# Gated recurrence: the next head's row projection placed between the last two half-size products, and the first head's ScalarE and VectorE work in another order

## What is computed

```
def c_layer(x, s0, w_in, norm_g, w_out, lb):
    q, f, i, g = jnp.split(jnp.einsum('btd,de->bte', x, w_in).astype(jnp.float32), 4, axis=-1)
    q = jax.nn.silu(q).reshape(B, T, H_C, C_DK)
    logf = jnp.logaddexp(jnp.log(lb), jnp.log1p(-lb) + jax.nn.log_sigmoid(f)).reshape(B, T, H_C, C_DK)
    k = -jnp.expm1(logf)
    v = i.reshape(B, T, H_C, C_DV)
    o, s_new = gla_chunked(q, k, v, logf, s0.astype(jnp.float32))
    o = o * lax.rsqrt(jnp.mean(jnp.square(o), axis=-1, keepdims=True) + RMS_EPS)
    o = o.reshape(B, T, D_MIX) * norm_g.astype(jnp.float32) * jax.nn.silu(g)
    return jnp.einsum('bte,ed->btd', o.astype(x.dtype), w_out), s_new
```

## Time and profile before

| | |
|---|---|
| median of 3 runs | 2076.14 us (2073.19 to 2078.51) |
| the profiled execution's own time | 2070.61 us |
| its span, first to last instruction | 2068.5 us |
| mean granted TensorE clock | 0.977 |
| TensorE busy | 1959.7 us, 95% of the span |
| VectorE, ScalarE, GpSimd busy | 1050.3, 773.6, 385.2 us |
| first and last row projection (L2254) | start at 1278.2 and 1884.2 us |

### The profile page before, as it was taken

How to read it: one execution, slowest core, us unless ns; L and a number is a source line. 1 busy time by engine, 2 the same in 40 slices (tenths; PEclk the granted TensorE clock), 3 DMA queues, 4 the chain that set the end, 5 groups by cost and what they waited for, 6 DMA issues and landing times. The chain is left out here.

```text
span 2068.5 us, 46493 instructions
## 1 busy us (share of the span) xinstructions
PE 1959.7 (95%) x19082; PEld 1470.9 (71%) x19082; DVE 1050.3 (51%) x2617; ACT 773.6 (37%) x1687; POOL 385.2 (19%) x424
## 2 busy tenths in 40 slices
PE   7999999989998999997997998899999999999998
PEld 7888888856666877875665444777888788788533
DVE  3211131158874444435774243667777877777332
ACT  0000011168774444342776010345445544544300
POOL 5432333336650000003541100000000000000000
PEclk9999999999998999998999998999999999999999
DMA  6334323453149999986663914499998998998730
GB/s 180 103 119 95 78 66 82 71 140 105 50 162 322 399 379 386 387 346 236 226 245 117 294 22 122 146 293 295 319 308 277 310 311 281 305 311 298 236 126 26
DMA packets 221953, 443.39 MB, mean 214 GB/s; under 512 B 60816, under 2 KB 182176, under 8 KB 205104
## 3 DMA queue, kind: packets, MB, share of 16 engines
q1 hardware_dynamic: 214288, 364.57, 55.0%
q0 software_dynamic: 7456, 75.86, 10.0%
HBM read 413.70 MB, written 165.23 MB: 280 GB/s over the span
## 5 line engine op out<-in xcount | busy, mean ns | idle before, releaser
L2264 PE MATMUL three<-x1T,arena 128*128 128x256 f32 x768 | 207.0, 397 | 3.7 <-DVE rec_qq L2655 3.7
L580 POOL TENSOR_TENSOR late<-late 128x512 f32<-128x512 f32 (+2 forms) x76 | 112.2, 1476 | 219.4 <-PE pab_bZ L368 126.4
L2563 POOL TENSOR_TENSOR rec_v_own<-rec_rows,row_own 64x512 f32<-64x512 f32 x16 | 16.6, 1040 | 729.7 <-PE rec_bX L2379 598.1
L2264 PEld LDWEIGHTS three<-x1T,arena 128*128 128x128 f32 x768 | 137.4, 193 | 19.1 <-DVE rec_qq L2655 4.1
L848 ACT ACTIVATE ap_sc<-ap_sc,ap_nmax 128x256 f32<-128x256 f32 (+1 forms) x192 | 106.3, 557 | 5.1 <-DVE ap_nmax L872 5.0
L1456 DVE COPY sa_kT<-sa_bT 128x512 f32<-128x512 f32 x80 | 55.2, 690 | 94.5 <-PE sa_bT L1312 94.4
L872 DVE CUSTOM_DVE_ANT_0 ap_sc<-ap_bS,ap_bias 128x256 f32<-128x256 f32 (+1 forms) x192 | 86.2, 486 | 14.0 <-DMA ap_bias<-in_bias_p 9.6
L907 POOL TENSOR_SCALAR ap_sc<-ap_sc,ap_rden,sgl 128x256 f32<-128x256 f32 (+3 forms) x128 | 76.8, 612 | 40.0 <-DVE ap_rden L880 39.7
L1456 ACT COPY sa_kT<-sa_bT 128x512 f32<-128x512 f32 x80 | 46.9, 586 | 98.8 <-PE sa_bT L1312 98.6
L1475 DVE COPY sa_xT<-sa_bT 128x512 f32<-128x512 f32 x64 | 43.8, 684 | 64.9 <-PE sa_bT L1377 64.5
L2264 PE MATMUL three<-rec_T,arena 128*128 128x256 f32 x256 | 63.8, 392 | 8.8 <-DVE rec_gg L2655 8.3
(11 more groups left out here) (505 smaller groups left out, 4583.4 us busy)
## 6 DMA issues: line engine op xcount, KB each, us to landing
out<-in_cache_a_k SPq DMA_DIRECT2D x8, 8160.0 KB, 30.0
out<-in_cache_a_v SPq DMA_DIRECT2D x8, 8160.0 KB, 29.6
arena<-in_cache_a_k SPq DMA_DIRECT2D x40, 1024.0 KB, 8.5
arena<-in_cache_a_v SPq DMA_DIRECT2D x40, 1024.0 KB, 9.1
arena<-in_w_in_c SPq DMA_DIRECT2D x64, 512.0 KB, 6.7
late<-in_w_in_ab SPq DMA_DIRECT2D x128, 64.0 KB, 2.4
late<-in_w_in_ab SPq DMA_DIRECT2D x8, 1024.0 KB, 5.3
ap_bias<-in_bias_p SPq DMA_DIRECT2D x16, 512.0 KB, 3.9
```

The source lines that it names most:

```text
L580: nc.gpsimd.tensor_tensor(to, a, b, op).then_inc(sums, 1)
L2264: last = nc.tensor.matmul(bank[:, 0:SEQ // 2], left[:, k, :], right[:, k, :], start=(first and k == 0), stop=(k == 3), skip_group_check=True)
L2563: nc.gpsimd.tensor_tensor(v_own[:, :, :], sV[h % 2].unsqueeze(1).broadcast_to([TS, HALF_NB, P]), row_own[:, :].unsqueeze(2).broadcast_to([ ...
```

## The change

Three edits, all in `recurrence`. TensorE does `project_rows(h + 1)` in iteration h, between A21 x B12 and A22 x T4 of `values_and_gates`, rather than at the start of iteration h+1; only `project_rows(0)` stays at a start. ScalarE does the first Exp (with its wait for `lb_ready`) behind the first head's side copy rather than ahead of everything. VectorE does, in the first head alone, the fifth `add`, then `set_constants`, then `forget`.

```diff
@@ values_and_gates
                     product(A21, B12, bR[0], True)
+                    if h + 1 < HC:
+                        project_rows(h + 1)
                     pe.wait_ge(added, ADDS * h + 9)
                     product(A22, T4, bR[0], False)
@@ TensorE's loop over the heads
-                    if before:
+                    if h == 0:
                         project_rows(h)
-                    else:
+                    if not before:
                         pe.wait_ge(added, ADDS * HC)
@@ ScalarE
                 act.wait_ge(const_ready, 16 * 6)
-                act.wait_ge(lb_ready, 1)
-                nc.scalar.activation(lb[:, :], one_lb[:, :], ACT.Exp).then_inc(lb_ready, 1)
                 line = Line(act, act_line)
@@
                         nc.scalar.copy(side[h % 2][:, :], bS[:, TS:4 * TS]).then_inc(side_read, 1)
+                        if h == 0:
+                            act.wait_ge(lb_ready, 1)
+                            nc.scalar.activation(lb[:, :], one_lb[:, :], ACT.Exp).then_inc(lb_ready, 1)
@@ VectorE
                         add(h, 4, 6, bR[0], qq[:, T_2], qq[:, T_2])
+                        if h >= 1:
+                            forget(h)
+                        dve.wait_ge(added, ADDS * h + 3)
+                        add(h, 5, 7, bR[0], qq[:, T_1], qq[:, T_1])
                         if h == 0:
                             set_constants()
-                        forget(h)
-                        dve.wait_ge(added, ADDS * h + 3)
-                        add(h, 5, 7, bR[0], qq[:, T_1], qq[:, T_1])
+                            forget(h)
                         forget_rest(h)
```

## The result

The changed kernel took 2116.99 us (median of 4 runs, 2109.74 to 2121.61) against 2074.8 us before (median of 4, 2073.19 to 2078.51). The ratio is 1.0198, with a 95% interval of 1.0179 to 1.0217: slower by some 41 us by the ratio, 42 by the medians. The profiled execution took 2109.74 us, with a span of 2107.6 us and a mean granted clock of 0.978; that is 39.1 us over the profiled execution of before in time and in span alike.

What follows compares the result with a forecast made beforehand. The prediction took TensorE to bound the steady heads. The profiled 2070.6 us plus 37.1 for 14 seams and 0 for the first head gave 2107.7; from the median 2076.1 it gave 2113 us, range 2103 to 2128.

Steps and rivals of the forecast that it cites:

- Step 1: At each seam the moved row projection waits 0.77 us for the bank ScalarE empties, replacing the old 0.52 us wait.
- Steps 2 and 3: At each seam A22 x T4 runs 3.85 us later and the tenth add 3.27 us later; S1 x T1 waits 1.20 us.
- Step 4: At each seam turn_values, no longer covered by the row projection, waits 1.20 us for ScalarE's logarithm.
- The sum of a seam: S1 x T1 starts 2.65 us later per head, at 14 seams: +37.1 us.
- The first head: Both small edits, their clock price and the seam from head 0 to 1: sum +0.4, taken as 0.
- -6.6: In the first head both edits together bring S4 x B22 from 1315.45 to about 1308.9.
- The worked gain of the two edits: First head: -3.8 us from the late Exp, -2.8 from the set-up order, +3.0 for low clock; -3.6 us.
- the first seam: From head 0 to 1 the tenth add and S1 come later, +2.3 us, with +1.7 us charged for low clock.
- The clock price behind the long wait: In the first head, +3.0 us for low clock behind a wait of some 5 us ahead of S4 x B22.
- The clock: Rival: three short waits per seam bring TensorE's clock down, +23.8 us at all 14 seams, 2137 us; chance 0.13.
- Sums not the last: Rival: at the seams only turn_values and turn_side wait, 1.48 us per head, +20.7 us: 2097 us; chance 0.04.
- The bubble is covered and nothing is late: Rival: the moved rows fill the 0.52 us wait, VectorE's late start is absorbed: faster, 2064.7 us; chance 0.03.

Runs made afterwards that it cites:

- bank_early: The whole change, with ScalarE's copy of the sample outputs moved ahead of the two exponentials: 2101.33 us against 2075.03 before, ratio 1.012.
- sums_early: The whole change, with VectorE making the next head's S1, S2 and S4 ahead of the tenth add: 2092.67 us against 2075.03 before, ratio 1.0078.
- turns_late: `sums_early` with TensorE doing turn_values behind A11 x B11 and turn_side behind S1 x T1: 2077.07 us against 2075.85 before, ratio 1.0.
- first_only: The whole change with the row projection put back, so only the first head's two edits: 2070.66 us against 2075.03 before, ratio 0.9976.
- exp_late: The kernel before with ScalarE's edit (the later Exp) alone: 2076.1 us in one execution, beside 2080.53 before.
- setup_late: The kernel before with VectorE's edit (fifth add, set_constants, forget) alone: 2071.99 us in one execution, beside 2080.53 before.
- all_early: `turns_late` with the early copy of the sample outputs of `bank_early`: 2064.54 us against 2075.85 before, ratio 0.9934.
- after_again: The changed kernel unaltered, measured once more: 2116.24 us against 2075.85 before, ratio 1.0183.

## Why the prediction was right, by its steps

**What bounds the kernel.** TensorE did, and each microsecond by which its work comes later at a seam was a microsecond of time. Seams of 42.64, 41.71, 41.35, 40.26, 39.72, 39.35 and 39.29 us go with ratios of 1.0183, 1.012, 1.0078, 1.0, 0.9976, 0.9934 and 0.9917. From the start of the recurrence to the last S1 x T1 the traces of these kernels differ from before by +39.6, +26.7, +16.7, +1.5, -5.3, -9.7 and -11.2 us (single stalls of TensorE that no other engine ends left out); the ratios give +38, +25, +16, 0, -5, -14 and -17. The last two agree less well than the others.

**Step 1, the rows' start.** Predicted a wait of 0.77 us for ScalarE's copy of the sample outputs; 0.85 measured, and taking it away gave back 0.93 us per seam (`bank_early`). ScalarE's copy starts 1616.56 - 1614.15 = 2.41 us behind A21 x B12, exactly as before (1600.08 - 1597.67), so nothing ahead of it depended on what was moved.

**Steps 2 and 3, the tenth add and the sums.** Predicted 5.02 us from the tenth add to the first sum, and the sum 0.06 us ahead of S1 x T1. The trace has 1627.63 - 1622.60 = 5.03 and 0.05. The wait itself was put at some 1.2 us and is shown as 1.03, since the profile counts idle time from the modelled end of turn_side (1626.93 + 0.41); from where turn_side's 0.21 us end it is 1.23. That this queue, and not the add's result, is what S1 x T1 waits for is shown by `sums_early`.

**Step 4, turn_values without its cover.** Predicted a wait of 1.20 us, measured 1.21. `turns_late` shows it to be a matter of order: with a product ahead of it the wait is gone.

**The sum of a seam** was put at 2.65 us and is 2.92. The term that was too small is the price of a handover, which was put at 0.06 us at every wait. That holds from VectorE to TensorE (1628.32 to 1628.37), from which it was taken; from ScalarE to TensorE it is 0.15 (the copy's end at 1616.75, the rows at 1616.90) and 0.14 (L2554's end at 1624.59, turn_values at 1624.73), and from the record's end of A22 x T4 to the tenth add 0.11 (1622.49 to 1622.60) instead of 0.04. From A21 x B12 to the rows it is 1616.90 - 1614.15 = 2.75 us where 2.66 were predicted; from the squares to turn_values 2.40, not 2.32; from A22 x T4 to the tenth add 2.10, not 2.03, which is on the way to the sums; and S1 x T1 with S2 x T2 behind a wait take 3.56 us to the next product instead of 3.46. The first, third and fourth lie one behind the other on the path to the end of S2 x T2: 0.09 + 0.07 + 0.10 = 0.26 of the missing 0.27. Over 14 seams this is 3.8 us, the difference between 37.1 and 40.9.

**The first head** was put at 0, out of -6.6, +3.0, +2.3 and +1.7. To S1 x T1 of the second head it was -2.6, and then +1.6 of low clock: -1.0. The 0 came near because terms cancelled. The worked gain of the two edits, -3.8 and -2.8 less 3.0 of clock, i.e. -3.6, was measured at -5.3 by `first_only` (-4.2 and -1.4 one by one, by `exp_late` and `setup_late`); the first seam was put at +2.3 and is +2.7 (47.2 less 44.5), of which 0.24 us is the wait of A11 x B11 that the working did not have; its low clock was put at +1.7 and is 1.6. The clock price behind the long wait, taken from the row after the 3.67 us wait, was the term that was most too high: in the changed kernel S4 x B22 and A21 x B12 took 5.3 us together behind the 4.77 us wait (1311.43 to 1316.76), 1.9 more than the usual 3.46, where 3.0 had been charged.

**The rivals.** *The clock* stayed at 1.00 through 500 us of seams with three waits each, so that rival is out for the profiled execution. The Trainium skill (TensorE: Matmul & The Clock Gate, "A second HAM failure mode: psum-queue depth-cycling") tells of a kernel in which frequent short idle times made the clock go up and down; by that rule it could have done so here, and this trace, with a clock of 1.00 at every seam, does not show it. It was at 0.50 within a microsecond of the end of each of the two waits over 3 us. *Sums not the last*: they were the last, by 1.03 us. *The bubble is covered and nothing is late* is what `all_early` had to be built for: it has the bank freed, the sums moved, and two transposes put behind products.

**The level.** 2113 was the median shown plus 37.1; with 3.8 more for the seams and 1.0 less for the first head it is 2116, and 2117 was measured. The executions reach from 2109.74 to 2121.61, so a level met to a microsecond is in part luck. Two executions of the changed kernel have a trace, of 2109.74 us and of 2118.12 (`after_again`). Their spans differ by 8.5 us, and 8.2 of them lie ahead of the recurrence, which starts at 1281.04 in the one and at 1289.25 in the other; from there to the last S1 x T1 they take 645.8 and 645.6 us.

## What to carry to other kernels

Before a block is moved forward to cover a gap, list what stood behind it and was covered by it: here 3.6 us of work moved across one product and left three other results uncovered, each by about a microsecond, and, as the runs that took them away one by one show, they added up. Compare the block's length with the gap: only as much as fits is free, and a single small matmul of later work filled the 0.52 us gap and cost nothing. An instruction that waits at the head of an in-order engine's queue delays all that is behind it; look at what that is rather than at who reads its own result.

## What the runs showed of the hardware beyond what was expected

A handover between engines can cost more than the idle time that the trace gives it. The wait for ScalarE's copy is shown as 0.85 us, and without it the seams came 0.93 us closer; S1 x T1 and S2 x T2 behind a wait are followed 3.56 us later by the next product, without one 3.46 (1609.07 to 1612.53 in the trace of before). The time between the end of another engine's record and TensorE's start depended on the engine: 0.05 us behind VectorE, 0.14 and 0.15 behind ScalarE.

TensorE's granted clock stayed at 1.00 with waits of 0.85, 1.21 and 1.03 us within 12 us, at each of 14 seams. It was at 0.50 behind a single wait of 3.01 us, and also, in the kernel before, from 1377 us on, behind a stall of 1.21 us in the midst of the pairs' narrow matmuls:

```profile
1377.00:1380.00 3.00, 2.82 (x12) 2.28 (x13) 0.85 (x4) 0.00 (x0) 0.00 (x0) 0.50 1.00 348
```

Other runs have such a stall at the same place of a head, and they do not agree. In `sums_early` it is shorter, 0.96 us, and the clock fell; in `first_only` it is longer, 1.44 us, and the clock stayed up (each time a row of the timeline, then one of the table by stretch):

```profile
1832.56 0.52 PE L2365 MATMUL rec_bA<-rec_far 128*16 128x16 f32 x7 [0.96 <-issue]
...
1833.00:1836.00 3.00, 3.00 (x9) 2.46 (x8) 0.85 (x4) 0.00 (x0) 0.00 (x0) 0.50 1.03 348
```

```profile
1375.12 0.52 PE L2363 MATMUL rec_bA<-rec_far 128*16 128x16 f32 x7 [1.44 <-issue]
...
1375.60:1378.00 2.40, 2.40 (x12) 2.14 (x12) 1.19 (x5) 0.00 (x0) 0.00 (x0) 1.00 1.03 354
```

So neither the length of a wait nor the matmuls round it tell by themselves whether the clock falls; what decides is open here. A price for low clock behind a wait, as the prediction charged it, is a chance and not a fixed sum.
